# Compressed keys and values ahead of the queries in the MLA low rank stage, and 512- and 256-key tiles that alternate in the GQA attention

## The reference

```python
out_x = sweep_query_blocks(lambda qb: attend(qb, k_all, v_all), qx)   # 512 keys
out_c = attend(qc, kc, vc)                                            # 256 keys
```

```python
cq, ckv, k_rope = jnp.split(h @ w_in, [384, 640], axis=-1)
q  = rms_norm(cq, q_norm_g)   @ w_uq      # 16 heads x 96
kv = rms_norm(ckv, kv_norm_g) @ w_ukv     # 16 heads x (64 + 64)
k_rope = apply_rope(k_rope, cos, sin)     # latent tokens
```

## Time and profile before

| what | before |
|---|---|
| median of 3 runs | 2164.83 us |
| the profiled execution, its time | 2163.54 us |
| its span in the trace | 2161.6 us |
| PE busy | 1984.5 us, 92% |
| DVE, ACT, POOL busy | 1042.7, 565.2, 59.4 us |
| mean granted TensorE clock | 0.964 of full speed |

### The profile page before, as it was taken

One profiled execution on the slowest core, in us unless ns is written; L12 is line 12 of the kernel. 1 busy time (PEld: TensorE's weight loads), 2 busy tenths in 40 slices (PEclk: granted clock), 3 DMA queues, 4 the chain that ended last, 5 costly groups with the idle time before them and its releaser, 6 DMA issues.

```text
span 2161.6 us, 27523 instructions
## 1 busy us (share of the span) xinstructions
PE 1984.5 (92%) x9979; PEld 1386.0 (64%) x9979; DVE 1042.7 (48%) x2206; ACT 565.2 (26%) x1176; POOL 59.4 (3%) x68
## 2 busy tenths in 40 slices
PE   6999898889889999979899899999999788999997
PEld 4888687657745555544355388888444355778886
DVE  3456662377332222235666877676787224423311
ACT  3333300171121111131174133332000124433410
POOL 0000000000000000000000001010000010000000
PEclk9999999989999999989899999999999888999999
DMA  9355382414559999530102312222674011134451
GB/s 389 140 208 216 142 335 88 161 55 193 210 199 426 425 424 419 219 136 0 39 1 103 131 61 95 78 96 112 265 264 176 0 55 47 40 117 153 144 203 44
DMA packets 39464, 357.25 MB, mean 165 GB/s; under 512 B 4295, under 2 KB 9038, under 8 KB 10318
## 3 DMA queue, kind: packets, MB, share of 16 engines
q1 hardware_dynamic: 39374, 356.04, 42.1%
HBM read 354.97 MB, written 1.05 MB: 165 GB/s over the span
## 4 chain that ended last, share of the span: by engine, by line
PE 86%; DVE 5%; ACT 2%; DMA 2%; issue 2%; DVEq 1%; PEldq 1%; PEld 1%; SPq 0%; ACTq 0%
PE bank L643 47%; PE bank L1299 12%; PE bank L1106 6%; PE bank L1091 3%; PE bank L1128 3%; PE bank L748 2%; PE bank L669 2%; PE bank L1271 2%; PE bank L1194 1%; DMA ring<-in_ada 1%; PE bank L1201 1%; ACT hn L1378 1%; DVE rstd L1834 1%; PE bank L1067 1%; DVE ring L1935 1%
## 5 line engine op out<-in xcount | busy, mean ns | idle before, releaser
L643 PE MATMUL bank<-hn,ring 128*128 128x256 f32 (+1 forms) x2080 | 520.4, 410 | 13.6 <-ACT hn L1378 9.7
L643 PE MATMUL bank<-arena,ring 128*128 128x256 f32 (+2 forms) x1600 | 470.4, 452 | 25.1 <-issue 13.1
L643 PEld LDWEIGHTS bank<-hn,ring 128*128 128x128 f32 x2080 | 399.1, 193 | 123.0 <-issue 67.8
L643 PEld LDWEIGHTS bank<-arena,ring 128*128 128x128 f32 (+1 forms) x1600 | 300.8, 190 | 190.8 <-issue 154.1
L1299 PE MATMUL bank<-hn,ring 128*128 128x256 f32 x704 | 161.0, 382 | 6.2 <-ACT hn L1378 6.2
L1299 PEld LDWEIGHTS bank<-hn,ring 128*128 128x128 f32 x704 | 134.6, 191 | 25.6 <-issue 7.0
L1814 DVE SCALAR_TENSOR_TENSOR bank<-ring,c_rows 128x1024 f32<-128x1024 f32 x96 | 118.1, 1230 | 34.2 <-DMA ring<-in_ada 29.2
L1299 PE MATMUL bank<-ring 128*128 128x256 f32 x528 | 122.9, 383 | 3.2 <-DVEq L2535 3.2
L1366 ACT ACTIVATE hn<-resid 128x256 f32<-128x256 f32 (+1 forms) x64 | 30.0, 492 | 349.8 <-DVE resid L1893 341.9
L1814 DVE SCALAR_TENSOR_TENSOR ring<-ring,c_rows 128x1024 f32<-128x1024 f32 x96 | 117.2, 1220 | 0.0
L1299 PEld LDWEIGHTS bank<-ring 128*128 128x128 f32 x528 | 100.9, 192 | 18.5 <-issue 3.9
(11 more groups left out here) (382 smaller groups left out, 2165.1 us busy)
## 6 DMA issues: line engine op xcount, KB each, us to landing
ring<-in_ada SPq DMA_DIRECT2D x28, 2048.0 KB, 8.2
ring<-in_up SPq DMA_DIRECT2D x44, 1024.0 KB, 4.9
ring<-in_egu SPq DMA_DIRECT2D x20, 2048.0 KB, 11.6
ring<-in_edn SPq DMA_DIRECT2D x39, 1024.0 KB, 10.2
ring<-in_down SPq DMA_DIRECT2D x16, 1408.0 KB, 9.5
arena<-in_egu SPq DMA_DIRECT2D x10, 2048.0 KB, 11.4
hn<-in_egu SPq DMA_DIRECT2D x9, 2048.0 KB, 11.6
ring<-in_adat SPq DMA_DIRECT2D x8, 2048.0 KB, 12.7
```

Source lines behind the costliest of these rows:

```text
L643: last = mm(out, lhs(i), rhs(i), start=i == 0, stop=i == k - 1)
```

## The change

GQA: the tiles of a block run in the order 0, 2, 1, 3 instead of 0, 1, 2, 3, so that tiles of 512 and 256 keys alternate; the widths that ACT and DVE use follow. MLA low rank: `ckv` and `k_rope` are multiplied first, each product announced by itself (`kv_mm`), and their norm and rotation are worked out while PE multiplies the query blocks; ACT squares each block as it is finished; the query norm follows. `end_phase()` no longer waits at the end of this stage (`end_phase(False)`). In each step of the head loop keys and values come first, the queries last; the first step waits for `ckvn` before its keys and for `cqn` before its queries.

```diff
-                    attention([gqa_pair(g, b, t) for g in range(KVG) for b in range(2) for t in range(4)], 4, 16, 8)
+                    attention([gqa_pair(g, b, t) for g in range(KVG) for b in range(2) for t in (0, 2, 1, 3)], 4, 16, 8)
...
+                    landed(1)
+                    for b in range(2):
+                        dot(bank[1 + 2 * b][:, :], lambda k: slot(1)[:, k * 288 + b * P:k * 288 + (b + 1) * P],
+                            lambda k: hn_block(k), KD).then_inc(s["kv_mm"], 1)
+                    dot(bank[2][ND:QK, :], lambda k: slot(1)[:, k * 288 + 256:k * 288 + 288], lambda k: hn[:, k, :], KD) \
+                        .then_inc(s["kv_mm"], 1)
+                    free(1)
                     landed(0)
                     for b in range(3):
-                        last = dot(bank[1 + b][:, 0:T], lambda k: slot(0)[:, k * 384 + b * P:k * 384 + (b + 1) * P],
-                                   lambda k: hn_block(k)[:, 0:T], KD)
...
-                    pe.wait_ge(s["kv_raw"], 2)
-                    dot(bank[0][:, 0:T], lambda b: ones, lambda b: cq_sq[:, b, :], 3)
-                    dot(bank[7][:, :], lambda b: ones, lambda b: ckv_sq[:, b, :], 2).then_inc(s["kv_rot"], 1)
-                    pe.wait_ge(s["kv_ready"], 2)
...
-                    end_phase()
+                        dot(bank[4 + b][:, 0:T], lambda k: slot(0)[:, k * 384 + b * P:k * 384 + (b + 1) * P],
+                            lambda k: hn[:, k, 0:T], KD).then_inc(s["kv_mm"], 1)
+                        if b == 0:
+                            pe.wait_ge(s["kv_raw"], 3)
+                            dot(bank[0][:, :], lambda x: ones, lambda x: ckv_sq[:, x, :], 2).then_inc(s["kv_rot"], 1)
+                        if b == 1:
+                            pe.wait_ge(s["kv_raw"], 4)
+                            mm(bank[2][ND:QK, 0:T], C("pmla")[ND:QK, ND:QK], kr_raw[ND:QK, 0:T], start=True, stop=True) \
+                                .then_inc(s["kv_dup"], 1)
+                    free(0)
...
+                    for b in range(3):
+                        pe.wait_ge(s["kv_raw"], 5 + b)
+                        last = mm(bank[7][:, 0:T], ones, cq_sq[:, b, :], start=b == 0, stop=b == 2)
+                    last.then_inc(s["kv_rot"], 1)
+                    end_phase(False)
...
+                            if not since(it, 1):
+                                pe.wait_ge(s["kv_ready"], 2)
                             dot(bank[b4 + 1][:, :], lambda k: ukv[:, k, 0, :], lambda k: ckvn[:, k, :], 2)
...
+                            if not since(it, 1):
+                                pe.wait_ge(s["kv_ready"], 3)
+                            for hh in range(2):
+                                last = dot(bank[b4][0:QK, hh * T:(hh + 1) * T], lambda k: uq[:, k, hh, :], lambda k: cqn[:, k, :], 3)
```

More of the change, by code:

```diff
@@ L621, in _, with end_phase @@
                 pe.sem_inc(slot_free[sl], 1)
-            def end_phase():
+            def end_phase(wait=True):
                 pe.drain().then_inc(phase, 1)
                 ended[0] += 1
-                pe.wait_ge(phase, 3 * ended[0])
+                if wait:
+                    pe.wait_ge(phase, 3 * ended[0])
             def landed(sl, i=0):
@@ L1352, in _, with end_phase @@
             fn = nc.scalar.activation
-            def end_phase():
+            def end_phase(wait=True):
                 act_e.drain().then_inc(phase, 1)
                 ended[0] += 1
-                act_e.wait_ge(phase, 3 * ended[0])
+                if wait:
+                    act_e.wait_ge(phase, 3 * ended[0])
             def sums(w, updated):
@@ L1644, in _ @@
                     end_phase()
-                    attention([Pair(branches=1, w=512 if t % 4 < 2 else 256) for t in range(32)], 16)
+                    attention([Pair(branches=1, w=512 if t % 2 == 0 else 256) for t in range(32)], 16)
                     end_phase()
                 else:
-                    act_e.wait_ge(s["kv_mm"], 2)
-                    for b in range(3):
[L1650 to L1657, removed]
+                    for b in range(2):
+                        act_e.wait_ge(s["kv_mm"], 2 + b)
+                        fn(ckv_sq[:, b, :], bank[1 + 2 * b][:, :], ACT.Square).then_inc(s["kv_raw"], 1)
+                    act_e.wait_ge(s["kv_mm"], 4)
+                    fn(kr_raw[ND:QK, :], bank[2][ND:QK, :], ACT.Copy).then_inc(s["kv_raw"], 1)
+                    act_e.wait_ge(s["kv_rot"], 2)
+                    fn(ckv_rstd[:, :], bank[0][:, :], ACT.Sqrt, scale=1.0 / KVL, bias=C("eps")).then_inc(s["kv_roped"], 1)
+                    for b in range(3):
+                        act_e.wait_ge(s["kv_mm"], 5 + b)
+                        fn(cq_sq[:, b, :], bank[4 + b][:, 0:T], ACT.Square).then_inc(s["kv_raw"], 1)
+                    act_e.wait_ge(s["kv_rot"], 3)
+                    fn(rstd[:, 0:T], bank[7][:, 0:T], ACT.Sqrt, scale=1.0 / QL, bias=C("eps")).then_inc(s["kv_roped"], 1)
+                    end_phase(False)
                     def heads(q, trip):
@@ L1779, in _, with end_phase @@
             ve.sem_inc(s["up_added"], 14)
-            def end_phase():
+            def end_phase(wait=True):
                 ve.drain().then_inc(phase, 1)
                 ended[0] += 1
-                ve.wait_ge(phase, 3 * ended[0])
+                if wait:
+                    ve.wait_ge(phase, 3 * ended[0])
             def ada_copy(b, c, buf):
@@ L2396, in _ @@
                     end_phase()
-                    attention([Pair(branches=1, w=512 if t % 4 < 2 else 256) for t in range(32)], 4, 16,
+                    attention([Pair(branches=1, w=512 if t % 2 == 0 else 256) for t in range(32)], 4, 16,
                               lambda g, b: V.tensor_copy(o2[:, g, :], b))
@@ L2404, in _ @@
                     ve.wait_ge(s["kv_roped"], 2)
-                    V.reciprocal(rstd[:, 0:T], rstd[:, 0:T])
                     V.reciprocal(ckv_rstd[:, :], ckv_rstd[:, :])
                     ve.drain()
-                    for b in range(3):
-                        V.scalar_tensor_tensor(cqn[:, b, :], bank[1 + b][:, 0:T], col("mla_q_norm_g_2", b), rstd[:, 0:T],
-                                               ALU.mult, ALU.mult)
                     for b in range(2):
-                        V.scalar_tensor_tensor(ckvn[:, b, :], bank[4 + b][:, :], col("mla_kv_norm_g_2", b), ckv_rstd[:, :],
+                        V.scalar_tensor_tensor(ckvn[:, b, :], bank[1 + 2 * b][:, :], col("mla_kv_norm_g_2", b), ckv_rstd[:, :],
                                                ALU.mult, ALU.mult)
@@ L2417, in _ @@
                     V.tensor_tensor(kr_roped[r, 0:T], kr_raw[r, 0:T], consts[r, CO["mcos"][0]:CO["mcos"][0] + T], ALU.mult)
-                    V.tensor_tensor(kr_roped[r, T:T2], bank[6][r, 0:T], consts[r, CO["msin"][0]:CO["msin"][0] + T], ALU.mult)
+                    V.tensor_tensor(kr_roped[r, T:T2], bank[2][r, 0:T], consts[r, CO["msin"][0]:CO["msin"][0] + T], ALU.mult)
                     ve.drain()
                     V.tensor_tensor(kr_raw[r, 0:T], kr_roped[r, 0:T], kr_roped[r, T:T2], ALU.add)
-                    end_phase()
+                    ve.wait_ge(s["kv_roped"], 3)
+                    V.reciprocal(rstd[:, 0:T], rstd[:, 0:T])
+                    ve.drain()
+                    for b in range(3):
+                        V.scalar_tensor_tensor(cqn[:, b, :], bank[4 + b][:, 0:T], col("mla_q_norm_g_2", b), rstd[:, 0:T],
+                                               ALU.mult, ALU.mult)
+                    ve.drain().then_inc(s["kv_ready"], 1)
+                    end_phase(False)
                     def heads(it, q):
```

15 lines of the change are left out of this document (2 added, 13 removed).

## The result

The changed kernel takes 2139.0 us, the median of four runs (2137.71 to 2143.7), against 2164.49 us for the kernel before in the same runs: ratio 0.9884, 95% interval 0.9872 to 0.9896. It is 25.5 us faster.

A forecast was written before the change was run, and what follows sets the result against it. TensorE's matmuls were taken as the bound (86% of the chain). Gains of 18.2 us (low rank) and 3.4 (GQA), 21.6 together, took 2163.54 to 2141.9; 1.3 for the median gave 2143.2 us, range 2139.5 to 2148.

The forecast's parts named there:

- the 0.5 and 0.4 us that I had given back: GQA attention: 0.5 us lost at the last wide tile, 0.4 at the start, taken off 4.3 us of saved stalls.
- Rival 2: GQA attention: alternation does nothing, ACT or DVE holds the period at 10.45 us; price 3.4 us, 2146.6 us; chance 0.09.
- the bound that I gave: Low rank stage: each of eight semaphore waits in PE's stream may cost 0.1 to 0.2 us, -1.5 us in all.
- the 5.2 that I had weighed against it: Low rank start: half clock might last 5.2 us instead of 3.35, making the gain 0.9 us less, 17.3 us.
- The thin cover of the query norm: First head step: keys and values hide the query norm with 0.3 us to spare; without them 3.7 us less gain.
- Rival 1: Low rank stage: query norm late, PE idle before the first queries; 2 us late gives 2144.9 us; chance 0.1.
- the third: Later work takes back part of the low rank gain; gain 12 to 15 us in all, 2150 to 2153 us; chance 0.06.
- theory C: Formed during the experiments: clock grid nearly fixed to program start; an idle TensorE stretch covering a grid step halves the clock.

The follow-up runs named there:

- gqa_alone: Kernel before with only the alternating tile order in the GQA attention; 2163.58 us, ratio 0.9988.
- before_again: Kernel before, unchanged, run and traced once more; 2165.05 us.
- shifted: Changed kernel with two extra matmuls on TensorE between the GQA attention and its output product; 2142.84 us.
- lowrank_alone: Kernel before with only the low rank and head loop part of the change, tiles in their old order; 2148.9 us, ratio 0.9918.
- query_norm_slow: Changed kernel with the query reciprocal taken three times instead of once on VectorE; one run, 2143.69 us.
- queries_first: Changed kernel with queries ahead of keys and values again in each head step; one run, 2146.64 us.
- phase_kept: Changed kernel with the waiting end_phase() at the end of the low rank stage; one run, 2148.16 us.
- filled_exp_early: Changed kernel with five extra matmuls around the MLA attention's start and a one-column exponential starting each attention; 2137.7 us, ratio 0.9866.
- after_again: Changed kernel, run and traced once more; 2138.96 us.

## Why the prediction was off

**GQA attention: right.** Period 9.83 (forecast 9.82), no wait, 3.6 us gained (3.4). Of the 0.5 and 0.4 us that I had given back, the 0.5 at the end is there as a wait of PE for DVE; the start gave back less than I had put. Rival 2 is out; `gqa_alone` has the gain by itself. (Rival 2 put both engines above 75% busy; DVE's 7.62 of 10.45 us are 73%.)

**Low rank stage: right, 0.7 us too much.** 17.5 instead of 18.2 us; the first block took 8.9 us (8.5), and the rest slipped by 0.1 to 0.2 us at a time where PE goes from one group of products to the next, inside the bound that I gave. The half clock after the first product lasted 3.5 us (to 1685.2), not the 5.2 that I had weighed against it. The thin cover of the query norm was real: DVE was done 0.2 us ahead of PE's need (0.3 forecast), and 3.5 us more on DVE became a wait of 3.38 us. Rival 1 did not occur.

**The step that failed** is the sum itself: "The change removes no matmul, so its whole worth is PE's idle time and half-clock time in the two stages." I carried everything behind the second head step over unchanged. But PE's clock in later stages depends on when their idle stretches fall. I had looked at the clock of the low rank stage and of the head loop, and put a price of 0.9 us on the moment of return there; the trace of the kernel before shows the same for the MLA attention, which runs there at a mean clock of 0.92, and I put it at nothing in my sum. Moved by some 20 us it ran at 0.97, and the stage took 4.4 us less, the feed-forward block 1.1 us less: 5.5 us, where the sum had 0. Of the forecast's rivals the third named "the clock falling at other points", as a loss only. The gain of the same size was missing; with it the forecast's low case is 2143.2 - 5.5 = 2137.7 us.

**How the total came out.** The gain between the two traces is 24.7 us against 21.6 in my sum: 5.5 more from the clock, 0.2 more from the tiles, 0.7 less from the low rank stage, and 1.8 less because the traced start was longer (3.1 in all, up to rounding). I had also added 1.3 us because the median of the kernel before lay that far above its traced execution. That execution had the short start of 1077.1 us (1079.0 in `before_again`); the traced execution of the changed kernel, with 1078.9, lay only 0.15 us below its median. So the miss of the median, 4.2 us, is smaller than the 5.5 us that the sum left out.

**What is shown and what not.** That those 5.5 us are clock is shown: same matmul counts, means of 0.92 and 0.97, and the five extra matmuls that take 5 us off the kernel before. That it is the moment and not the change is shown by `shifted`, and by the traces side by side. Counted from the first score of the GQA attention, the MLA attention begins

| after | in | takes |
|---|---|---|
| 704.0 us | changed kernel, both traces | 65.4 us |
| 707.0 | `shifted` | 68.3 |
| 707.5 | `lowrank_alone` | 70.0 |
| 709.0 to 709.1 | `query_norm_slow`, `queries_first`, `phase_kept` | 66.6 each |
| 721.6 | `gqa_alone` | 69.8 |
| 725.0 | kernel before, both traces | 69.8 |

Equal moments gave equal times. Why an idle stretch of some length lowers the clock in one place and not in another is not settled: `lowrank_alone` starts its attention 3.5 us later than the changed kernel, with the same idle stretches of 1.0 and 2.1 us ahead of it, and took 70.0 us. Its clock fell 2.2 us ahead of the first score, that of the changed kernel only 1.3 us behind it. The windows (start and end, length, busy time of each engine, clock), first of the changed kernel, then of `lowrank_alone`, whose first scores are at 1782.90 and 1786.45:

```profile
1784.30:1787.50 3.20, 3.20 (x5) 1.35 (x4) 1.22 (x1) 0.64 (x1) 0.00 (x0) 0.50 0.00 0
```

```profile
1784.30:1791.00 6.70, 4.62 (x7) 1.97 (x7) 2.55 (x4) 0.00 (x0) 0.00 (x0) 0.50 0.00 0
```

In the changed kernel the clock thus fell while PE was in the scores, not in an idle stretch. The half of theory C that says that the clock halves where an idle stretch covers a step of its grid does not hold as it was put.

## What to carry to other kernels

Work out a change at its own place, then ask of each later stage with idle stretches at its start what it costs at either level of TensorE's clock, and put that difference into the range on both sides: here 5.5 us, a fifth of the whole gain. Test two parts of a change apart and together; where the sum does not add up, compare stages that the diff does not touch. A norm chain on VectorE and ScalarE can be hidden by putting products that do not need it ahead, and when the cover is as thin as here, any time added to the chain shows at once, with the clock's fall on top.

## What the hardware did that I had not expected

The half-clock stretches came back at the same places of a kernel's own course: 69.8 us for the attention in both traces of the kernel before and in `gqa_alone`, 65.4 in both of the changed kernel, though the two executions of the kernel before reached the GQA attention 1.9 us apart. It goes further: in 13 of the 14 traces the clock rose to 2.4 GHz 12.4 us after the first score of the GQA attention, within 0.05 us, and in the fourteenth (`filled_exp_early`, where PE waited less there) 9.0 us after it. So the steps of the clock kept their place against that attention, not against the start of the program. The Trainium skill says, on the page "TensorE: Matmul & The Clock Gate", section "What's actually happening", that the monitor runs free and its phase varies from run to run; these traces show less of that than the page leads one to expect. One run of `lowrank_alone`, 6 us below the others, may be such a case.

A VectorE operation waited for GpSimd. In the first head step of the changed kernel the operation on two SBUF operands that takes 0.69 us in every other step took 2.52, while GpSimd's second copy ran to 1730.22. It took 2.56 in `after_again` and `lowrank_alone`, and 0.69 in the kernel before, where the copies end ahead of it. The timeline:

```profile
1726.62 3.60 POOL L1755 COPY arena<-ring 32x4096 f32<-32x4096 f32 x1
...
1728.23 2.52 DVE L2447 TENSOR_TENSOR ring<-ring 96x512 f32<-96x512 f32 x1 [5.33 <-ACT ring L1682]
...
1735.32 0.69 DVE L2447 TENSOR_TENSOR ring<-ring 96x512 f32<-96x512 f32 x1 [0.29 <-issue]
```

The Trainium skill has this on the page "SBUF — State Buffer", section "Who interferes with whom": a VectorE operation with two inputs in SBUF contends with a GpSimd operation that reads SBUF, and the one that issues later is blocked until the other has finished. The trace agrees: GpSimd ended at 1730.22, VectorE at 1730.75, 0.53 us later, somewhat less than its usual 0.69. PE did not wait for it: the first rotation, at 1732.44, has no idle time ahead of it in the timeline of the result.
